# The stretch from the second norm to the first expert pair in a new order, with the normalised x gathered, and the last scatter by column halves

## The chip, the core and the metric

The kernel runs on one core of a Trainium2 chip. Its engines work beside each other, each through its own list of instructions: PE (TensorE, matrix products), DVE (VectorE), ACT (ScalarE), POOL (GpSimd), and SP (SyncE), which issues most of the transfers. They wait for one another by semaphores. The metric is the device time of one execution in microseconds (us), as a median of repeated runs.

## The reference

One decoder layer for 256 tokens with 1024 features: a mixer (a state-space branch and differential attention), cross-attention into 256 memory tokens, and a mixture of 64 experts. After each part x is normalised. What the change touches is the last third, cut here to what is computed:

```python
x = layer_norm(alpha * x + cross_attention(x, mem), ln2_g, ln2_b)       # the second norm
scores = sigmoid(x @ w_router); choice = scores + router_bias           # 64 experts in 8 groups of 8
grp_score = sum of the 2 largest choices in each group                  # the best 4 groups stay
idx = top 8 of choice inside those groups
gates = scores[idx] / sum(scores[idx]) * 2.5
y = (silu(x @ w_sh[:, :256]) * (x @ w_sh[:, 256:])) @ w_sh_down         # the shared expert
for e in range(64):
    gu = x @ w_gu[e]
    y += gates[:, e] * ((silu(gu[:, :256]) * gu[:, 256:]) @ w_down[e])
out = layer_norm(alpha * x + y, ln3_g, ln3_b)                           # the third norm
```

All numbers are float32. Where precision needs it, a float32 operand is split into a rounded part (`_hi`, `h`) and the rest (`_lo`, `l`), which PE multiplies in its faster form.

## The kernel before, in words

The tokens are two blocks of 128 (`TB`). PE goes through a fixed list of outputs, each 256 columns wide, in four PSUM banks S[0] to S[3] in turn (the tile name `stream` in the trace); four more banks W[0] to W[3] (`work`) take everything else. In the part that matters the order is written out by hand:

1. **Output projection** of the cross-attention, `token_major("co", k)`, eight outputs: the token block changes fastest, then the column block. DVE adds each to x (`add_output`, L1222) and takes statistics. When a token block is complete, DVE and ACT form its deviation (`variance`, `norm_sqrt`) and DVE normalises x in place (`normalise`, L1233, tile `xres`).
2. PE turns the normalised x of each token block (`turn`, L1747). Behind each turn it runs 13 products whose result nobody reads (`keep_warm`, L1587). ACT and DVE leave the turned x with the norm's gain and bias as `x2T` (L881, L1294).
3. **Router**: eight products for both token blocks at once (L1795), sigmoid on ACT, a turn on PE (L1802), and then the selection on DVE (L1307 to L1334), which ends with `sel`. Four products count the selected tokens (L1812), DVE makes places and one-hot matrices from the counts (L1350 to L1360). Meanwhile PE has the **shared expert's** four outputs (`token_major("sh", k)`, L1580).
4. In token layout, x gets its gain and bias by two operations a block: block 0 on DVE (`gain_bias`, L1251, L1252), block 1 on GpSimd (L652, L654). ACT rounds it (`x2h`, L891), DVE takes the rest (`x2l`, L1302).
5. **Gather**: products of `x2h`, `x2l` with the one-hot matrices (`gather`, L1827 to L1833) bring x to the experts' slots; ACT and DVE copy eight blocks out to `xg`. The products of the shared expert are turned in between (`turn_shared`, L1819).
6. **Pairs**: 32 pairs of experts. Of each, 32 records of gate and up (L1879), the scatter of the pair before (L1868; in pair 0 the shared expert's second product, L1854), turns, two blocks of the next gather, and the down products (L1903). ACT makes silu and `yh`, DVE `yl`. Pair 0 also adds the residual to the W banks (L1453, L1454), and ahead of it DVE lists overflow items (L1411 to L1427), which are none for this input.
7. **End**: the last scatter, the sums, and the third norm, whose first token block goes mainly through DVE and whose second goes through ACT (L946 to L956) and DVE (L1504 to L1511); two stores.

The expert weights come as 96 tiles of 2 MB in halves of 1 MB, on SP's queue, into a ring of 8 places (`places`). Place 6 is `place_w` and `place_x`; `place_x` shares its bytes with `xres`. Refills wait for PE's gate-up and down products (`refill`).

## Time and profile before

| | us |
|---|---|
| median of 3 runs (1011.42 to 1011.84) | 1011.68 |
| the profiled execution | 1012.25 |
| its span, first to last instruction | 1010.2 |
| PE busy | 987.0 |
| DVE busy | 517.0 |
| ACT busy | 382.7 |
| moved by DMA | 292.43 MB |

Times inside the trace count from the start of the span. The page gives busy time by engine; the chain of waits follows the end of the program back through what released what; a timeline lists the instructions of one engine in order, with the idle time ahead of each in brackets. "x8" behind a row is the number of instructions merged in it. The granted clock (PEclk) is a share of TensorE's full speed: 1.00 is 2.4 GHz, 0.50 is 1.2 GHz. PE, DVE and ACT work on different tiles at once, so a row's duration is only on the path where another engine waits for it.

### The profile page before, as it was taken

What the parts mean: (1) busy time and instruction counts of PE and PEld (TensorE: products, weight loads), DVE (VectorE), ACT (ScalarE), POOL (GpSimd) and SP (SyncE); (2) the same over time, 40 slices, a digit from 0 to 9 for tenths busy, and PEclk for the clock granted to TensorE, in tenths of its full rate; (3) what the DMA queues carried; (4) which work ended last, traced back from release to release, by engine and by line L of the source; (5) the groups of instructions that cost most, each with busy time, mean ns of one, the idle gap of its engine ahead of it and who ended that gap; (6) DMA issues with size and microseconds to landing.
All of it is one profiled execution on the core that took longest, in us unless ns stands there. A gap on an engine that the chain in (4) does not pass through costs nothing.

```text
span 1010.2 us, 15434 instructions
## 1 busy us (share of the span) xinstructions
PE 987.0 (98%) x6362; PEld 708.3 (70%) x6363; DVE 517.0 (51%) x1024; ACT 382.7 (38%) x705; POOL 58.6 (6%) x56
## 2 busy tenths in 40 slices
PE   8999999999999999999999999999999999999994
PEld 7999999999999999998874444444444444444332
DVE  5888456757589967845775232222223222322223
ACT  6776435555577735445321121111111111211112
POOL 0001103333200000000200000000000000000000
PEclk9999999999999999999999999999999999999998
DMA  7585534333344556559757999999999999999972
GB/s 295 189 307 181 194 128 165 126 125 126 126 170 164 195 182 227 190 209 390 277 208 286 416 420 419 420 420 420 420 420 420 419 420 421 421 419 420 420 320 84
DMA packets 42694, 292.43 MB, mean 289 GB/s; under 512 B 4728, under 2 KB 6912, under 8 KB 7936
## 3 DMA queue, kind: packets, MB, share of 16 engines
q1 hardware_dynamic: 41840, 286.19, 71.4%
q0 software_dynamic: 784, 5.24, 1.4%
q8 instruction: 51, 0.84, 0.3%
q14 instruction: 19, 0.16, 0.0%
HBM read 290.36 MB, written 2.63 MB: 290 GB/s over the span
## 4 chain that ended last, share of the span: by engine, by line
PE 94%; DVE 3%; ACT 1%; DMA 1%; issue 0%; SPq 0%; ACTq 0%
PE stream L1555 32%; PE stream L1879 22%; PE stream L1903 11%; PE stream L1580 8%; PE work L1868 7%; PE stream L1827 2%; PE stream L1831 1%; PE stream L1829 1%; PE stream L1833 1%; PE work L1678 1%; PE work L1654 1%; PE work L1854 1%; PE work L1767 1%; PE work L1781 1%; PE work L1666 1%; PE stream L1896 1%
## 5 line engine op out<-in xcount | busy, mean ns | idle before, releaser
L981 DVE TENSOR_TENSOR w_lo<-raw,w_hi 128x1024 fp32r<-128x1024 f32 x142 | 172.0, 1231 | 55.9 <-ACT w_hi L677 55.8
L1879 PE MATMUL stream<-ring,xg 128*64 128x512 f32 x640 | 197.0, 592 | 0.8 <-issue 0.8
L677 ACT ACTIVATE w_hi<-raw 128x1024 fp32r<-128x1024 f32 x142 | 147.1, 1052 | 61.3 <-DMA raw<-in_wdense 44.6
L1555 PE MATMUL stream<-xT_hi,w_hi 128*128 128x256 f32 x560 | 159.4, 285 | 0.0
L1555 PE MATMUL stream<-xT_lo,w_hi 128*128 128x256 f32 x560 | 157.9, 282 | 0.0
L1555 PE MATMUL stream<-xT_hi,w_lo 128*128 128x256 f32 x560 | 157.8, 282 | 0.0
L1879 PEld LDWEIGHTS stream<-ring,xg 128*64 128x64 f32 x640 | 63.0, 137 | 91.6 <-issue 90.4
L1555 PEld LDWEIGHTS stream<-xT_hi,w_hi 128*128 128x128 f32 x560 | 106.1, 190 | 3.7 <-issue 3.1
L1555 PEld LDWEIGHTS stream<-xT_hi,w_lo 128*128 128x128 f32 x560 | 105.9, 189 | 0.0
L1555 PEld LDWEIGHTS stream<-xT_lo,w_hi 128*128 128x128 f32 x560 | 105.6, 189 | 0.0
L1432 DVE TENSOR_TENSOR hh<-h,stream 128x256 f32<-128x256 f32 x32 | 13.5, 422 | 172.3 <-ACT h L910 172.3
L1459 DVE SCALAR_TENSOR_TENSOR yl<-stream,slot_gate,yh 128x512 fp32r<-128x512 f32 x64 | 48.0, 751 | 91.6 <-ACT yh L922 91.6
L910 ACT ACTIVATE h<-stream 128x256 f32<-128x256 f32 x32 | 12.3, 384 | 199.6 <-PE stream L1879 199.6
L922 ACT ACTIVATE yh<-stream,slot_gate 128x512 fp32r<-128x512 f32 x64 | 44.0, 687 | 101.0 <-PE stream L1903 101.0
L1903 PE MATMUL stream<-ring,hT 128*64 128x512 f32 x320 | 73.1, 598 | 1.3 <-DVE scatT L1439 1.3
L1879 PE MATMUL stream<-place_e,xg 128*64 128x512 f32 x128 | 56.2, 592 | 0.0
L1868 PE MATMUL work<-yh,scatT 128*128 128x512 f32 x128 | 53.7, 420 | 1.6 <-DVE yl L1459 1.6
L1868 PE MATMUL work<-yl,scatT 128*128 128x512 f32 x128 | 50.4, 394 | 0.0
L1903 PEld LDWEIGHTS stream<-ring,hT 128*64 128x64 f32 x320 | 21.2, 136 | 40.5 <-issue 34.3
L1868 PEld LDWEIGHTS work<-yh,scatT 128*128 128x128 f32 x128 | 24.0, 187 | 31.8 <-issue 25.1
L913 ACT ACTIVATE xg<-stream 128x512 f32<-128x512 f32 x28 | 16.7, 598 | 77.5 <-PE stream L1833 77.5
L1012 DVE SCALAR_TENSOR_TENSOR acc<-xpad,cs,acc 128x256 f32<-128x256 f32 x72 | 34.8, 484 | 2.4 <-ACT acc L713 0.7
(378 smaller groups left out, 2034.4 us busy)
## 6 DMA issues: line engine op xcount, KB each, us to landing
ring<-in_wstream SPq DMA_DIRECT2D x120, 1024.0 KB, 14.9
raw<-in_wdense SPq DMA_DIRECT2D x73, 1024.0 KB, 4.8
place_e<-in_wstream SPq DMA_DIRECT2D x24, 1024.0 KB, 16.0
place_m<-in_wstream SPq DMA_DIRECT2D x12, 1024.0 KB, 13.2
place_c<-in_wstream SPq DMA_DIRECT2D x12, 1024.0 KB, 14.9
place_w<-in_wstream SPq DMA_DIRECT2D x12, 1024.0 KB, 14.4
place_x<-in_wstream SPq DMA_DIRECT2D x12, 1024.0 KB, 16.0
ln<-in_lnp POOLq DMA_DIRECT2D x3, 1024.0 KB, 6.9
```

What stands on the lines that cost most here:

```text
L677: nc.scalar.activation(w_hi[:, q % ROUNDED, :], raw[:, q % 6, :], ACT.Copy).then_inc(w_rounded, 1)
L913: nc.scalar.activation(feature_block((pair // 4 + 1) % 2, 2 * (pair % 4)), S[1][:], ACT.Copy).then_inc(gath_act, 1)
L922: nc.scalar.activation(yh[:, c * 512:(c + 1) * 512], (S[3], S[1])[c][:], ACT.Copy, scale=slot_gate[:, 0:1]).then_inc(yh_done, 1)
L981: tt(w_lo[:, q % 6, :], raw[:, q % 6, :], w_hi[:, q % ROUNDED, :].bitcast(F32), ALU.subtract).then_inc(w_rest, 1)
L1012: ins = stt(acc[:, b % 2, :], xpad[:, b % 4, j:j + SEQ], conv_w[:, b, j:j + 1], acc[:, b % 2, :], ALU.mult, ALU.add)
L1459: stt(yl[:, c * 512:(c + 1) * 512], (S[3], S[1])[c][:], slot_gate[:, 0:1], yh[:, c * 512:(c + 1) * 512].bitcast(F32), ALU.mult, ALU.subtra ...
L1555: last = mm(S[n % 4][:, 0:SEQ], w[:, b, :], a[:, kb, :], start=(kb + j == 0), stop=(kb == chunks * KB - 1 and j == len(parts) - 1))
L1580: last = mm(S[n % 4][:, 0:SEQ], a[:, kb, rows], w[:, cols, :], start=(kb + j == 0), stop=(kb == KB - 1 and j == len(parts) - 1))
L1827: mm(by_expert[:, :, window[0]], x2h[:, 0, w], onehot[:, buf, 0, :, window[0]], start=True, stop=False, skip_group_check=True)
L1868: last = mm(W[2 * t + c][:], scatT[:, t * P:(t + 1) * P], y[:, c * 512:(c + 1) * 512], start=False, stop=False, skip_group_check=True)
L1879: last = mm(S[2][e * SLOTS:(e + 1) * SLOTS, :], feature_block(buf, kb)[:, col + e * SLOTS:col + (e + 1) * SLOTS], tiles[e][kb // 4][:, kb ...
L1903: last = mm((S[3], S[1])[c][e * SLOTS:(e + 1) * SLOTS, :], hT[:, kb, e * SLOTS:(e + 1) * SLOTS], tile[e][:, o:o + 512], start=(kb == 0), s ...
```

## The change

The edits, most of them between the second norm and the first pair:

- The output projection runs its eight outputs in another order (`ORDER`), so that token block 0 is complete at the sixth. The turn of block 0 stands inside the eighth output, the turn of block 1 inside the shared expert's first output. The shared expert's outputs are ordered by token block. `keep_warm` is gone from here.
- The router's products are made for each token block by itself, in two bands of the array, four features' blocks each; a product with a matrix of two identities adds the bands and turns the scores. The sigmoid comes after that.
- The gathered x is the normalised x without gain and bias (`xn_hi`, `xn_lo`). Gain and bias are applied when ACT and DVE leave the gathered banks (`leave_gathered`). The token layout gets its gain and bias on DVE just ahead of pair 0; GpSimd has no part in it any more.
- The selection has fewer operations (one masked operation for both blocks, one product with `lower8`).
- The count stands inside the shared expert's last output. DVE makes the gates after the one-hots.
- The first gather takes its banks in another order (`first_banks`); the first half of the first pair waits for four of the eight blocks.
- The residual is added in four operations rather than eight. The list of overflow items moves behind pair 1.
- The first half of expert tile 6 is loaded earlier, its second half after the residual. The shared expert's second weight (`wsd`) is loaded once the last shared output is done, to other bytes.
- In each pair ACT copies the turned h ahead of the gathered block.
- The last scatter goes by column halves. A root of one element is computed in the last pair, ahead of `yh`.
- The third norm's second block is subtracted, scaled and stored by halves.

```diff
+ORDER = {"co": [(0, 0), (1, 0), (0, 1), (1, 1), (0, 2), (0, 3), (1, 2), (1, 3)],
+         "sh": [(0, 0), (0, 1), (1, 0), (1, 1)]}
...
+    return ORDER[kind][k] if kind in ORDER else (k % TB, k // TB)
...
+        DONE.append(OUT0[_k] + 1 + (last_output(_k, _m, _q // 2) if _k in TOKEN_MAJOR else _q // _c))
...
-            sp.wait_ge(split_l, 2)
-            expert_halves(6, 6)
+            expert_half(6, 6, 0)
             sp.wait_ge(proj_ready, DONE[-1])
             expert_halves(7, 7)
...
+                if pair == 0:
+                    sp.wait_ge(residual_done, 4)
+                    expert_half(6, 6, 1)
...
+            for c in range(2):
+                cols = slice(c * 512, (c + 1) * 512)
+                sp.wait_ge(ln_done, TB + 2 + c)
+                sp.dma_start(out[0, P:SEQ, cols], normed[:, 1, cols]).then_inc(stored, 16)
...
-            nc.gpsimd.tensor_tensor(xres[:, 1, :], xres[:, 1, :], ln2[:, 0, :], ALU.mult).then_inc(norm_pool, 1)
...
+            pool.wait_ge(proj_ready, DONE[-1])
             pool.dma_start(wsd[:], wshd).then_inc(wsd_ld, 16)
...
+                if t == 0:
+                    round_x(0)
...
+            round_x(1)
+            act.wait_ge(router_mm, 2)
+            nc.scalar.activation(scoresT[:], W[0][:, 0:SEQ], ACT.Copy).then_inc(score_sig, 1)
+            act.wait_ge(router_mm, 3)
+            nc.scalar.activation(scores[:], W[3][:, 0:TB * EXPERTS].rearrange("p (t e) -> p t e", t=TB), ACT.Sigmoid
+                                 ).then_inc(score_sig, 1)
...
+            def leave_gathered(buf, kb, bank):
+                nc.scalar.activation(feature_block(buf, kb), bank[:], ACT.Identity, scale=gain2[:, kb:kb + 1],
+                                     bias=gain2[:, KB + kb:KB + kb + 1]).then_inc(gath_act, 1)
...
+                if pair == PAIRS - 1:
+                    nc.scalar.activation(half_var[:, 1:2], ones[:, 0:1], ACT.Sqrt)
...
+            add_output("co", {6: lambda: normalise(1, 0).then_inc(xhat_done, 1), 7: lambda: leave_x2T(0)})
+            normalise(1, 1).then_inc(xhat_done, 1)
+            leave_x2T(1)
...
-            link(ts(gmask[:], goff[:], TOP_GROUPS - 0.5, None, ALU.is_lt))
-            link(ts(goff[:], gmask[:], -MASKED, MASKED, ALU.mult, ALU.add))
-            for t in range(TB):
-                by_group = masked[:, t].rearrange("p (g e) -> p g e", g=EGROUPS)
-                link(tt(by_group, choice[:, t].rearrange("p (g e) -> p g e", g=EGROUPS),
-                        gmask[:, t].unsqueeze(2).to_broadcast([P, EGROUPS, 8]), ALU.mult))
-                link(tt(by_group, by_group, goff[:, t].unsqueeze(2).to_broadcast([P, EGROUPS, 8]), ALU.add))
+            link(ts(gmask[:], goff[:], TOP_GROUPS - 0.5, 0.5, ALU.is_lt, ALU.subtract))
+            link(stt(masked[:].rearrange("p t (g e) -> p t g e", g=EGROUPS),
+                     gmask[:].unsqueeze(3).to_broadcast([P, TB, EGROUPS, 8]), -4.0 * MASKED,
+                     choice[:].rearrange("p t (g e) -> p t g e", g=EGROUPS), ALU.mult, ALU.min))
...
+            shared_product(0)
+            ve.wait_ge(router_mm, 4)
...
+            shared_product(1)
...
+            def gain_bias(t):
+                link(tt(xres[:, t, :], xres[:, t, :], ln2[:, 0, :], ALU.mult))
+                link(tt(xres[:, t, :], xres[:, t, :], ln2[:, 1, :], ALU.add))
+            ve.wait_ge(ln_ld, 32)
+            for t in range(TB):
+                gain_bias(t)
...
-                            link(stt(bank, x2h[:, t, cols].bitcast(F32), ALPHA, bank, ALU.mult, ALU.add))
-                            stt(bank, x2l[:, t, cols].bitcast(F32), ALPHA, bank, ALU.mult, ALU.add
-                                ).then_inc(residual_done, 1)
+                            stt(bank, xres[:, t, cols], ALPHA, bank, ALU.mult, ALU.add).then_inc(residual_done, 1)
...
+                if pair == 1:
+                    list_items()
...
+                    if t:
+                        ve.wait_ge(norm_act, 5 + c)
...
+            subtract_third_mean(1)
+            ve.wait_ge(ln_sqrt, 2 * TB + 2)
+            link(nc.vector.reciprocal(rstd[:, 1:2], half_var[:, 0:1]))
+            for c in range(2):
+                cols = slice(c * 512, (c + 1) * 512)
+                stt(normed[:, 1, cols], normed[:, 1, cols], rstd[:, 1:2], ln3[:, 1, cols], ALU.mult, ALU.add
...
-                keep_warm(S[0][:, 0:SEQ], ocT_r[0][:, 0, 0:P], ocT_r[0][:, 1, :], 13)
...
+            def scores_of(t):
+                pe.wait_ge(x2T_act, 4 * t + 4)
+                pe.wait_ge(x2T_dve, 4 * t + 4)
+                for step in range(4):
+                    for band in range(2):
+                        kb = 4 * band + step
+                        last = mm(W[0][band * EXPERTS:(band + 1) * EXPERTS, t * P:(t + 1) * P], w_router[:, kb, :],
+                                  x2T[:, kb, t * P:(t + 1) * P], start=(step == 0), stop=(step == 3))
+                last.then_inc(router_mm, 1)
...
+                    last = mm(W[3][:, t * EXPERTS:(t + 1) * EXPERTS], scoresT[:, t * P:(t + 1) * P], two_ident[:],
+                              start=True, stop=True)
...
+            for k in range(8):
+                token_major("co", k, ocT_r, ready=(cav_rest, 2) if k == 0 else None,
+                            midway={1: lambda: turn_normed(0)} if k == 7 else {})
+            scores_of(0)
+            token_major("sh", 0, x2T, midway={6: lambda: turn_normed(1)})
+            token_major("sh", 1, x2T, midway={3: lambda: scores_of(1), 6: turn_scores})
             token_major("sh", 2, x2T)
-            pe.wait_ge(sel_done, 1)
-            for k, (w, t) in enumerate(((tri, 0), (tri, 1), (ones, 0), (ones, 1))):
-                last = mm(W[2][:, k * EXPERTS:(k + 1) * EXPERTS], w, sel[:, t, :], start=True, stop=True)
-            last.then_inc(router_mm, 1)
-            token_major("sh", 3, x2T)
+            token_major("sh", 3, x2T, midway={4: count_selected})
...
+                if kb in (0, 2):
+                    turn_shared(kb // 2)
                 elif kb >= 4:
                     pe.wait_ge((gath_act, gath_dve)[kb % 2], (kb - 4) // 2 + 1)
-                gather(kb, S[kb % 4], 0)
+                gather(kb, first_banks[kb], 0)
...
+                    if pair % 4 == 0:
+                        pe.wait_ge(gath_act, 2 + pair + 2 * half)
+                        pe.wait_ge(gath_dve, 2 + pair + 2 * half)
...
+            def scatter_half(c, y):
+                for t in range(TB):
+                    mm(W[2 * t + c][:], scatT[:, t * P:(t + 1) * P], y[:, c * 512:(c + 1) * 512], start=False, stop=False,
+                       skip_group_check=True)
+            pe.wait_ge(yl_done, 2 * PAIRS - 1)
+            scatter_half(0, yh)
+            scatter_half(0, yl)
+            pe.wait_ge(yh_done, 2 * PAIRS)
+            scatter_half(1, yh)
             pe.wait_ge(yl_done, 2 * PAIRS)
-            scatter()
+            scatter_half(1, yl)
```

Where the instructions move, two places on PE and one on ACT. On PE, between the output projection and the shared expert, before (L1747 turns x, L1587 is the part nobody reads, L1795 the router, L1580 the shared expert, `ocT` the input of the output projection):

```order
L1747 MATMUL work<-cs,xres 128x128 [waits xhat_done,dve_took]
L1747 MATMUL work<-cs,xres 128x128 x7
L1587 MATMUL stream<-ocT_hi 128x256 x13
L1747 MATMUL work<-cs,xres 128x128 [waits xhat_done]
L1747 MATMUL work<-cs,xres 128x128 x7
L1587 MATMUL stream<-ocT_hi 128x256 x13
L1795 MATMUL work<-x2T,cs 64x256 [waits x2T_dve,x2T_act]
L1795 MATMUL work<-x2T,cs 64x256 x7
L1580 MATMUL stream<-raw,x2T 128x256 [waits dense_ld0,dve_took]
L1580 MATMUL stream<-raw,x2T 128x256 x3
L1802 MATMUL work<-cs,scoresT 128x64 [waits score_sig]
L1802 MATMUL work<-cs,scoresT 128x64
```

And now, from the first router products on (L1830); the turn of block 0 is further up, inside the last output of the projection:

```order
L1830 MATMUL work<-x2T,cs 64x128 [waits x2T_dve,x2T_act]
L1830 MATMUL work<-x2T,cs 64x128 x7
L1616 MATMUL stream<-raw,x2T 128x256 [waits dense_ld0,dve_took]
L1616 MATMUL stream<-raw,x2T 128x256 x3
L1616 MATMUL stream<-raw,x2T 128x256 [waits dense_ld0]
L1616 MATMUL stream<-raw,x2T 128x256
L1783 MATMUL work<-cs,xres 128x128 [waits xhat_done]
L1783 MATMUL work<-cs,xres 128x128 x7
L1616 MATMUL stream<-raw,x2T 128x256 x2
L1616 MATMUL stream<-raw,x2T 128x256 [waits dense_ld1,dve_took]
L1616 MATMUL stream<-raw,x2T 128x256 x2
L1830 MATMUL work<-x2T,cs 64x128 [waits x2T_dve,x2T_act]
```

The router's products are half as wide and come twice, each between pieces of other products, and both turns have moved into such pieces.

On PE, from the count of the selected to the gather, before (L1812 the count, L1580 the last shared output, L1819 the turn of the shared product) and, in the second piece, now (L1844, L1616, L1859):

```order
L1812 MATMUL work<-sel,cs 128x64 [waits sel_done]
L1812 MATMUL work<-sel,cs 128x64 x3
L1580 MATMUL stream<-raw,x2T 128x256 [waits dve_took]
L1580 MATMUL stream<-raw,x2T 128x256 x7
L1819 MATMUL work<-cs,hh 128x128 [waits sh_done,split_l,onehot_done]
L1819 MATMUL work<-cs,hh 128x128
L1827 MATMUL stream<-onehot,x2h 128x8x48 [waits sh_silu]
```

```order
L1616 MATMUL stream<-raw,x2T 128x256 x3
L1844 MATMUL work<-sel,cs 128x64 [waits sel_done]
L1844 MATMUL work<-sel,cs 128x64 x3
L1616 MATMUL stream<-raw,x2T 128x256 x4
L1859 MATMUL work<-cs,hh 128x128 [waits sh_done,split_l,onehot_done]
L1859 MATMUL work<-cs,hh 128x128
L1867 MATMUL stream<-onehot,xn_hi 128x8x48
```

The count is inside an output, and the gather's first blocks no longer wait for ACT's second silu.

On ACT, from the last pair's silu to the end, before and now (`half_var` of L943 is the root of one element; the rows between the branches, which run only for overflow items, are among them):

```order
L910 ACTIVATE h_191<-stream 128x256 [waits gu_mm]
L916 ACTIVATE hT<-stream 128x256 [waits hT_mm]
L922 ACTIVATE yh<-stream,slot_gate 128x512 [waits down_mm,gate_cp]
L922 ACTIVATE yh<-stream,slot_gate 128x512 [waits down_mm]
...
L929 ACTIVATE h_191<-stream 128x256 [waits o_gu]
...
L946 ACTIVATE unread,half_sum<-work 128x512 [waits moe_mm]
L946 ACTIVATE unread,half_sum<-work 128x512 [waits norm_act]
L948 ACT_TABLE_LOAD [waits ln_var]
L948 ACTIVATE rstd<-rvar 128x1 [waits norm_act]
L949 ACTIVATE half_sum<-half_sum 128x1
```

```order
L934 ACTIVATE h_193<-stream 128x256 [waits gu_mm]
L936 ACTIVATE hT<-stream 128x256 [waits hT_mm]
L943 ACT_TABLE_LOAD
L943 ACTIVATE half_var<-cs 128x1
L947 ACTIVATE yh<-stream,slot_gate 128x512 [waits down_mm,gate_cp]
L947 ACTIVATE yh<-stream,slot_gate 128x512 [waits down_mm]
...
L954 ACT_TABLE_LOAD
L954 ACTIVATE h_193<-stream 128x256 [waits o_gu]
...
L971 ACT_TABLE_LOAD
L971 ACTIVATE unread,half_sum<-work 128x512 [waits moe_mm]
L971 ACTIVATE unread,half_sum<-work 128x512 [waits norm_act]
L973 ACT_TABLE_LOAD [waits ln_var]
L973 ACTIVATE rstd<-rvar 128x1 [waits norm_act]
```

There is a table load ahead of the root of one element, one inside the branch, one ahead of the first sum (L971), and one ahead of the root of the third norm (L973), where before there was one, at L948.

## Rows read from the trace of the kernel before

**Rows 1.** The page: busy time, share of the span and instructions of each engine.

```profile
PE 987.0 (98%) x6362; PEld 708.3 (70%) x6363; DVE 517.0 (51%) x1024; ACT 382.7 (38%) x705; POOL 58.6 (6%) x56
```

**Rows 2.** Windows: stretch, length, busy us by engine, PEclk, DMA share, GB/s.

```profile
700.00:714.50 14.50, 14.50 (x70) 6.62 (x69) 4.50 (x12) 2.63 (x5) 0.00 (x0) 1.00 1.02 422
...
1003.00:1006.00 3.00, 0.00 (x0) 0.00 (x0) 1.93 (x4) 0.94 (x4) 0.00 (x0) 0.50 0.43 175
```

**Rows 3.** Chain of waits, output projection: start us, us, what.

```profile
471.51 22.42 PE stream L1580 x192
```

**Rows 4.** Timeline of PE: start us, us, engine, line, op, out<-in, shapes [idle before].

```profile
494.01 1.07 PE L1747 MATMUL work<-cs,xres 128*128 128x128 f32 x8
494.83 1.80 PE L1587 MATMUL stream<-ocT_hi 128*128 128x256 f32 x13
...
505.12 8.90 PE L1580 MATMUL stream<-raw,x2T 128*128 128x256 f32 x40
513.86 1.00 PE L1812 MATMUL work<-sel,cs 128*128 128x64 f32 x8
514.70 3.67 PE L1580 MATMUL stream<-raw,x2T 128*128 128x256 f32 x16
...
520.86 0.44 PE L1819 MATMUL work<-cs,hh 128*128 128x128 f32 x2 [0.51 <-DVE hh L1383]
...
521.84 0.34 PE L1827 MATMUL stream<-onehot,x2h 128*128 128x384 f32 x1
...
525.39 0.35 PE L1827 MATMUL stream<-onehot,x2h 128*128 128x384 f32 x1
...
527.09 1.47 PE L1879 MATMUL stream<-ring,xg 128*64 128x512 f32 x5 [0.83 <-issue]
```

**Rows 5.** Groups by line, PE: xcount | busy us, mean ns | idle.

```profile
L1678 PE MATMUL work<-dec,xsdt 128*64 128x128 f32 x128 | 8.8, 279 | 0.0
```

**Rows 6.** Timeline of DVE from the second norm to the one-hots.

```profile
493.95 0.42 DVE L1222 SCALAR_TENSOR_TENSOR xres<-xres,stream 128x256 f32<-128x256 f32 x1
...
495.85 0.81 DVE L1233 TENSOR_SCALAR xres<-xres,mv,rstd 128x1024 f32<-128x1024 f32 x1 [0.27 <-ACT rstd L841]
...
501.48 3.25 DVE L1252 TENSOR_TENSOR xres<-xres,ln 128x1024 f32<-128x1024 f32 x1
...
505.44 0.28 DVE L1308 TENSOR_TENSOR choice<-work,row 128x128 f32<-128x128 f32 x1
...
509.24 0.17 DVE L1325 TENSOR_SCALAR goff<-gmask 128x16 f32<-128x16 f32 x1
...
511.65 0.23 DVE L1334 TENSOR_SCALAR sel<-choice 128x128 f32<-128x128 f32 x1
...
513.34 1.22 DVE L1302 TENSOR_TENSOR x2l<-xres,x2h 128x1024 fp32r<-128x1024 f32 x1
...
515.16 0.22 DVE L1350 TENSOR_SCALAR over<-work 128x64 f32<-128x64 f32 x1
...
516.32 1.03 DVE L1360 TENSOR_TENSOR onehot<-cs,slot_of 128x384 fp32r<-128x384 f32 x2
```

**Rows 7.** All transfers of L514 from 519 us on: issue to landing.

```profile
DMA to landing us min/median/max: 4.8/15.2/24.7
```

**Rows 8.** Chain of waits at the end, and the page's row on the stores.

```profile
994.13 0.70 ACT yh L922
...
995.66 2.13 PE work L1868 x8
...
999.90 1.28 ACT L948
...
1004.03 1.41 DVE normed L1504 x2
...
1005.55 1.28 DVE normed L1511
...
out_dram<-normed SPq DMA_DIRECT2D x2, 512.0 KB, 2.6
```

263 lines of the change are left out of this document (114 added, 149 removed).

## The prediction

> **What bounds the kernel now.** I read the page first: PE is busy 987.0 of 1010.2 us [rows 1], so only the places where PE waits, or does work that can go, are worth anything. Then the table of windows: a stretch inside the 32 expert pairs shows PE busy 14.50 of 14.50 us while the DMA share is 1.02 at 422 GB/s [rows 2]. That is two limits almost at once, and I return to it. Then the chain of waits [rows 3]: the output projection of the cross-attention starts at 471.51 and holds it for 22.42 us. The first expert product starts at 527.09 [rows 4]. The changed stretch is these 55.6 us. Last the timelines of PE and DVE between these marks [rows 4, 6]. DVE goes without a break from the router's scores (choice at 505.44) over the selection (sel at 511.65), the places (515.16) and the one-hot matrices (516.32), and PE can begin its gather only when DVE and ScalarE have handed over everything. So between the second norm and the gather a chain through DVE sets the time, not PE.
>
> **The stretch, rebuilt step by step.** I lay PE's new program on the clock of the profiled execution.
>
> The output projection: 22.42 us from 471.51 [rows 3] ends at 493.93. The new order of its eight outputs finishes the first 128 tokens at output 5. In the trace the add of a last column block starts at 493.95 and the normalised x of that token block ends at 496.66 (495.85 + 0.81) [rows 6]: 2.71 us of DVE and ScalarE. From the end of output 5 (493.93 minus two outputs of 2.80, 22.42 / 8, is 488.33) that gives 491.1, and PE wants it at 491.5, one eighth into output 7. So the turn of x (eight transposes) goes inside output 7 without a wait. It costs PE 0.82 (from 494.01 to the next product at 494.83 [rows 4]): 494.75. ScalarE rounds x first and then leaves its four x2T blocks, which I estimate at 2.5 us together, by 493.7, before PE asks.
>
> Scores of the first half: eight products of 64 weight columns by 128, in two bands of the array. The trace has this very shape: x128 in 8 batches, 8.8 us busy [rows 5], 1.10 a batch. To 495.85. In the kernel before all eight came as 256-column products, after both halves were ready. Lower bound 0.87 (pairs of products on the two bands side by side at full overlap), upper bound 1.75 (no overlap).
>
> Shared expert, output 0: records follow each other at 0.2185 us (8.74 us for 40, from 505.12 to 513.86) [rows 4], 16 of them are 3.5; with the second turn inside, 500.15. The second half of x is normalised 2.71 after 494.8, at 497.5; PE asks at 498.5. Output 1: 3.5, plus 1.10 for the second scores, plus the product that adds the two bands and turns the scores. That product is half of the four at 513.86 (0.84 to the next row at 514.70), 0.42. It ends at 505.15. Outputs 2 and 3 up to the middle: 508.65, 510.4.
>
> Does the selection keep up? PE is at the second scores at 501.45 and leaves them at 502.55; ScalarE copies them (0.4), then must load the sigmoid's table, 1.28 us by the load at 999.90 [rows 8]; it stands behind the copy, where before it stood ahead of the wait for the scores. That ends near 504.3, while PE has turned the scores at 504.25. Sigmoid 0.4: DVE starts choice at about 504.75, 0.7 earlier than 505.44. From there to sel before: 511.65 + 0.23 - 505.44 = 6.44. Gone are five small links (four masked operations and goff, from 509.24 to 510.49, now one operation of 0.3) and one geq link (0.2): -1.15. So sel is ready at 510.05; PE reaches the count at 510.4. A margin of 0.35 us, thin. Before, the DVE work that followed sel (gates, one x2l of 1.22 at 513.34, zeros) sat ahead of the places; now it is done while DVE waited for scores, or behind the one-hots.
>
> Count 0.84: 511.25. Places and one-hots: 515.16 to 516.32 and 1.03 more [rows 6], 2.2 us: 513.5. PE ends the last shared output at 513.0, so a wait of 0.5 us stays. Gather: a transpose pair with its block costs 0.98 (520.86 to 521.84), a block alone 0.71 (five blocks from 521.84 to 525.39) [rows 4]. Two by 0.98 and six by 0.71 is 6.2: 519.7. The first expert product then waited 0.83 us for the last gathered blocks to leave their banks [rows 4]; now it asks for four of the eight, long done, and for the others 3.4 us later. Leaving a bank now multiplies and adds the norm's gain; it is off the path with 0.5 us or more at each bank. Start of the first pair: 519.7. **Saved: 527.09 - 519.7 = 7.4 us.**
>
> **Inside the pairs** nothing is gained: PE issues the same products, 14.50 of 14.50 busy. In pair 0 DVE now does gain and bias on x (four operations) where it listed the overflow items. Before, such an operation took 3.25 us at 501.48, with GpSimd working on the other half of x; the subtraction of the same size took 1.22 at 513.34, with GpSimd idle [rows 6]. I take 1.22, 4.9 us in all, and the list that leaves was about as long. At 3.25 each it would be 13, and h would be late by about 2 us for PE in pair 0. The Trainium skill (SBUF — State Buffer, Who interferes with whom) says that a DVE operation with two SBUF inputs and a GpSimd one that reads SBUF lock each other out; by that rule the new place, with GpSimd idle, is cheap. Residual adds halve, four by 0.7.
>
> The transfers: half of expert tile 6 now goes into the bytes of x, so it is issued only after the residual adds. By pairs of 14.5 us [rows 2] and about 5.5 more in pair 0 for the shared product, that is some 20 us behind pair 0's start (my estimate), and pair 2 needs it 3.4 us into its own products, at 29 + 5.5 + 3.4 = 38. Landings took 4.8 to 24.7 us in this stage, median 15.2 [rows 7]: 15.2 leaves 3 us, and at that point of the stage the queue is still short. Value: nothing; bound: 24.7 gives a wait of 6.7. The queue also carries 1 MB more (2.5 us at 422 GB/s) while it is nearly full.
>
> **The end.** The last scatter was eight products behind the last yl, from 995.66, 2.13 us with the two that close the sums [rows 8]. Six of the eight now need only what is there before, and two are left: at about 0.235 each (2.13 less 0.25 for the closing two, by eight) six are 1.4. The third norm's second half: its two subtractions (1.41 at 1004.03) now start one by one behind the squares and are done at about the time the root ends, and the last scaling (1.28 at 1005.55) is cut in two of 0.65, the same in sum: 1.41 less the reciprocal and a link is 1.05 gained. The last store is 256 KB in place of 512 KB at 2.6 us [rows 8]; between nothing and half of it I take 0.4. **The table of the root:** the title says that it is loaded in the last pair. Yet the order of ScalarE's instructions shows behind it a load ahead of the copy that sums (L971) and again one ahead of the root (L973), as before at 999.90, 1.28 us. So this gains nothing, and adds one load of 1.28, which fits: from ScalarE's last yh (994.13 + 0.70 [rows 8]) with a branch to about 996.2, against the banks ready at 997.8 - 1.4 = 996.4. The Trainium skill (ScalarE activation tables: per-element evaluation and per-set limits, Table sets in the compiler and the runtime) says that loads are placed per block, which agrees with that order: a branch stands between. Another page of the Trainium skill (ScalarE: Activation LUTs, What ACT_TABLE_LOAD costs) adds a drain of 1.38 us to each load; by it the end would be some 0.7 later; the chain of waits has nothing but the load's 1.28 there, and speaks against it. **Saved at the end: 1.4 + 1.05 + 0.4 = 2.8 us.**
>
> **Sum.** 7.4 + 2.8 = 10.2. The profiled execution took 1012.25 (span 1010.2 and 2.0 around it), 0.57 above the median of the runs, so it goes to 1002.05 and the median from 1011.68 to **1001.5**.
>
> **Rivals.**
> - The selection is late. If DVE misses the count slot (margin 0.35), all behind it slips: scores without overlap (+1.3), or a slower chain. Time 1002.5 to 1004. For it: three hand-overs on ScalarE and PE within 3 us. Against: PE then also has less to wait for.
> - The transfers become the bound. A wait in pair 2 for tile 6, up to 6.7, or late in the stage, where the rate of 422 GB/s (14.9 us for the 6.29 MB of a pair) is below PE's 14.5: the lead shrinks each pair. Time 1003 to 1008.2.
> - Pair 0's DVE work is late (2 us): 1003.5.
> - The root's load does leave the path: 1.3 less, 1000.2. The order speaks against it.
> - **Slower than before:** the 26 warming products (L1587) go. If PE's clock fell to its lower level (the granted clock is 0.50 at 1003 to 1006, when PE had been idle since its last product near 997.8 [rows 2, 8]) through a gap at the one-hots, the work under it would double: one pair adds 14.5 us, and from 10.2 us of work at half clock the change loses; 1016 with one pair. Against: the granted clock is 1.00 before inside the pairs, which follow a gap of 0.83 us and one of 0.51 [rows 2, 4], and the new waits are no longer.
>
> **How the numbers follow.** Forecast 62%; selection late 17%; transfers 8%; pair 0 late 4%; load gone 5%; clock 2%; and 2% that nothing of it comes through (1011.7). The range of 8 in 10: from 1000.2 (load gone, scores at their lower bound) to 1005.0 (selection late and a part of the transfers). A measurement tells 0.2%, 2.0 us, from no change. Faster 96%, same 2%, slower 2%.
>
> **What would show it.** The first L1918 product near 519.7; the first gathers with about 0.5 us of idle time, released by the one-hots; no idle time at the count; no wait for DMA at pair 2; PE 14.5 a pair; two loads of 1.28 on ScalarE behind the last yh; the two last products at 0.1 behind yl; the last store about 8 us behind the banks (before 1005.55 + 1.28 against 997.8, 9.0). It is wrong if PE waits at the count, at a bank in the gather or in the pairs, or if the clock falls.

## The result, and the profile after

The changed kernel took 1002.50 us (median of four runs, 1001.78 to 1003.16) against 1011.71 for the kernel before (four runs, 1011.42 to 1011.84): ratio 0.9901, 95% interval 0.9880 to 0.9922. The forecast was 1001.5 with a range from 1000.2 to 1005.0. It was faster, as forecast, by 9.2 us where I had said 10.2.

The page of the changed kernel, against [rows 1]: the span is 10.4 us shorter, PE's busy time 6.2.

```profile
span 999.8 us, 15421 instructions
...
PE 980.8 (98%) x6354; PEld 702.5 (70%) x6355; DVE 517.1 (52%) x1019; ACT 392.1 (39%) x709; POOL 53.0 (5%) x54
```

The two profiled spans do not differ by the change alone. The start of PE's timeline (columns: start us, us, engine, line, op, out<-in, shapes, x instructions, [idle before]), before and after:

```profile
6.60 5.77 PE L1555 MATMUL stream<-xT,raw 128*128 128x256 f32 x14 [0.80 <-DMA raw<-in_wdense]
```

```profile
6.48 5.85 PE L1591 MATMUL stream<-xT,raw 128*128 128x256 f32 x25 [0.67 <-DMA raw<-in_wdense]
```

Both rows stop at 12 us, where the view's window ends. The code is the same there, but up to that mark PE has started 14 products in one case and 25 in the other. The trace's record of the granted clock says why: it rises from 0.50 to 1.00 (1.2 to 2.4 GHz) at 11.66 us before and at 5.82 us after. Up to the output projection that leaves the two kernels 1.38 us apart, a matter of the run and not of the change, as more traces show below.

The stretch on PE, to be held against [rows 4]:

```profile
490.10 1.03 PE L1783 MATMUL work<-cs,xres 128*128 128x128 f32 x8
...
493.51 1.09 PE L1830 MATMUL work<-x2T,cs 128*64 128x128 f32 x16
494.54 2.86 PE L1616 MATMUL stream<-raw,x2T 128*128 128x256 f32 x12
497.23 1.04 PE L1783 MATMUL work<-cs,xres 128*128 128x128 f32 x8
...
500.36 1.09 PE L1830 MATMUL work<-x2T,cs 128*64 128x128 f32 x16
...
502.78 0.55 PE L1837 MATMUL work<-two_ident,scoresT 128*128 128x64 f32 x4
503.18 6.26 PE L1616 MATMUL stream<-raw,x2T 128*128 128x256 f32 x28
509.27 1.00 PE L1844 MATMUL work<-sel,cs 128*128 128x64 f32 x8
510.11 1.95 PE L1616 MATMUL stream<-raw,x2T 128*128 128x256 f32 x8
512.56 0.44 PE L1859 MATMUL work<-cs,hh 128*128 128x128 f32 x2 [0.51 <-DVE onehot L1379]
...
518.83 5.37 PE L1918 MATMUL stream<-ring,xg 128*64 128x512 f32 x24
```

Read the start and the brackets. PE goes from the output projection, whose last output holds the turn at 490.10, through scores, shared expert and count (509.27) to the gather with one idle time only, 0.51 us for the one-hot matrices at 512.56. Where [rows 4] had 0.83 us ahead of the first pair, the first pair starts at 518.83 with none. VectorE, to be held against [rows 6]:

```profile
503.69 0.29 DVE L1333 TENSOR_TENSOR choice<-scores,row 128x128 f32<-128x128 f32 x1 [1.07 <-ACT scores L906]
...
508.66 0.23 DVE L1354 TENSOR_SCALAR sel<-choice 128x128 f32<-128x128 f32 x1
...
510.31 0.23 DVE L1369 TENSOR_SCALAR over<-work 128x64 f32<-128x64 f32 x1 [0.97 <-PE work L1844]
...
511.48 1.03 DVE L1379 TENSOR_TENSOR onehot<-cs,slot_of 128x384 fp32r<-128x384 f32 x2
...
523.58 1.22 DVE L1431 TENSOR_TENSOR xres<-xres,ln 128x1024 f32<-128x1024 f32 x1
...
528.61 1.03 DVE L1379 TENSOR_TENSOR onehot<-cs,slot_of 128x384 fp32r<-128x384 f32 x2
529.56 0.41 DVE L1462 TENSOR_TENSOR hh<-h,stream 128x256 f32<-128x256 f32 x1
```

Now the selection waits for its input (1.07 us at 503.69) and the places for the count (0.97 at 510.31): the chain through VectorE stands beside PE's work. It is done with sel at 508.89 (508.66 + 0.23), 0.38 us before PE starts the count. Gain and bias take 1.22 us each at 523.58, as in the subtraction at 513.34 of [rows 6] and not as at 501.48. The second group's one-hots and h (528.61, 529.56) follow.

The tail, against [rows 8]:

```profile
983.42 2.75 PE L1942 MATMUL stream<-ring,hT 128*64 128x512 f32 x12
...
987.12 0.63 PE L1987 MATMUL work<-yh,scatT 128*128 128x512 f32 x2
987.12 1.28 ACT L971 ACT_TABLE_LOAD   x1 [0.22 <-issue]
...
987.74 0.72 PE L1987 MATMUL work<-yl,scatT 128*128 128x512 f32 x2
...
989.02 0.38 PE L1900 MATMUL work<-onehot,turner 128*128 128x2 f32 x2 [0.56 <-issue]
...
991.39 1.28 ACT L973 ACT_TABLE_LOAD   x1 [0.54 <-DVE rvar L1237]
...
992.99 1.28 DVE L1541 SCALAR_TENSOR_TENSOR normed<-normed,rstd,ln 128x1024 f32<-128x1024 f32 x1 [0.37 <-ACT rstd L973]
...
995.95 1.42 DVE L1547 SCALAR_TENSOR_TENSOR normed<-normed,rstd,ln 128x512 f32<-128x512 f32 x2
996.73 0.99 SPq L621 DMA_DIRECT2D out_dram<-normed  x2
```

The two last scatter products (987.74) stand 0.05 us behind the last yl, but ahead of the closing sums is an idle time marked issue, 0.56 us at 989.02. Behind its last yh ScalarE loads two tables, one at 987.12 under cover and one at 991.39 on the chain of waits.

From the marks of the two traces (first product of the output projection, of the first pair, end of the last down product, end of the span) the difference of 10.42 us divides so. (The first product has its own record a little ahead of the merged row: 471.16 against the 471.51 of [rows 3].)

| stretch | before | after | gain | forecast |
|---|---|---|---|---|
| start to output projection | 471.16 | 469.78 | 1.38 | 0 |
| output projection to first pair | 55.93 | 49.04 | 6.89 | 7.4 |
| pairs, to the end of the last down product | 466.99 | 467.34 | -0.35 | 0 |
| tail | 16.15 | 13.65 | 2.50 | 2.8 |
| of it: from the last down product to the end of the closing sums | 3.82 | 3.24 | 0.58 | 1.4 |
| third norm, to VectorE's last instruction | 8.93 | 7.96 | 0.97 | 1.05 |
| last store | 3.41 | 2.45 | 0.96 | 0.4 |

What went from PE in the stretch can be counted in the two traces. Two rows of the timeline before and one of its chain of waits belong to it:

```profile
497.57 1.79 PE L1587 MATMUL stream<-ocT_hi 128*128 128x256 f32 x13
...
519.24 0.41 PE L1819 MATMUL work<-cs,hh 128*128 128x128 f32 x2 [0.87 <-DVE hh L1383]
```

```profile
499.37 3.64 PE work L1795 x16
```

From the start of each record to the start of the next, the 26 unread products took 3.6 us and are gone; the router's products took 3.57 and take 2.05, 1.5 less; and PE's idle time falls from 2.4 us (0.1, 0.1, 0.87, 0.51, 0.83) to 0.51, 1.9 less. That is the 6.9 us, but for 0.1. So most of it is work that PE no longer does. No run puts the unread products back, so their price by itself is read from the rows and not measured.

### The profile page after: what moved, and what is told of

Its sections match the earlier page's. It is cut to its first block, busy times and chain, and to the rows that moved or that the text cites. A ratio compares the mean times of both kernels' runs of the same rounds, so it can differ in the third digit from the quotient of the medians.

```text
span 999.8 us, 15421 instructions
## 1 busy us (share of the span) xinstructions
PE 980.8 (98%) x6354; PEld 702.5 (70%) x6355; DVE 517.1 (52%) x1019; ACT 392.1 (39%) x709; POOL 53.0 (5%) x54
## 4 chain that ended last, share of the span: by engine, by line
PE 95%; DVE 2%; DMA 1%; ACT 0%; issue 0%; SPq 0%; DVEq 0%; ACTq 0%
PE stream L1591 32%; PE stream L1918 22%; PE stream L1942 11%; PE stream L1616 9%; PE work L1907 6%; PE stream L1867 2%; PE stream L1871 1%; PE stream L1869 1%; PE stream L1873 1%; DMA raw<-in_wdense 1%; PE work L1714 1%; PE work L1690 1%; PE work L1893 1%; PE work L1803 1%; PE work L1817 1%; PE work L1702 1%
## 5 line engine op out<-in xcount | busy, mean ns | idle before, releaser
L936 ACT ACTIVATE hT<-stream 128x256 f32<-128x256 f32 x32 | 12.3, 384 | 92.1 <-PE stream L1935 92.1
L1404 DVE TENSOR_SCALAR xg<-stream,gain 128x512 f32<-128x512 f32 x32 | 25.8, 810 | 23.2 <-PE stream L1873 23.2
## 6 DMA issues: line engine op xcount, KB each, us to landing
place_m<-in_wstream SPq DMA_DIRECT2D x12, 1024.0 KB, 15.2
```

Source lines behind the costliest of these rows:

```text
L1404: return ts(dst, src, gain2[:, kb:kb + 1], gain2[:, KB + kb:KB + kb + 1], ALU.mult, ALU.add)
```

## The experiments

All kernels of a group ran on one chip with runs of the kernel before. The differences asked for are mostly one or two us, and the runs of one kernel lie 0.2 to 1.5 us apart, in seven of the kernels (before among them) 2 to 4.4, so each verdict goes by the marks of its one trace, and the time stands beside it. The columns below are those of the table above. Beside the tail, the stretch alone, the early count and the 6 products, before took 1012.13 us (13 runs); in the two other groups 1011.87 and 1011.89 (7 each).

| kernel | time, median (range) | full clock from | projection starts | stretch | pairs | tail |
|---|---|---|---|---|---|---|
| before | 1011.71 | 11.66 | 471.16 | 55.93 | 466.99 | 16.15 |
| changed | 1002.50 | 5.82 | 469.78 | 49.04 | 467.34 | 13.65 |
| tail alone | 1009.86 (1008.89 to 1010.37) | 10.92 | 470.73 | 55.93 | 467.30 | 13.89 |
| stretch alone | 1005.02 (1004.10 to 1006.73) | 6.47 | 469.80 | 49.09 | 467.35 | 15.78 |
| count of items early | 1001.79 (1000.99 to 1001.92) | 10.24 | 470.50 | 49.08 | 467.28 | 12.84 |
| 6 products at the start | 1001.91 (1001.73 to 1001.94) | 7.37 | 469.96 | 48.96 | 467.35 | 13.65 |
| root behind the branch | 1001.58 (1001.42 to 1002.32) | 5.63 | 469.69 | 49.11 | 467.36 | 13.22 |
| no root in the pair | 1002.41 (1001.89 to 1003.33) | 10.29 | 470.55 | 49.04 | 467.34 | 13.64 |
| selection later | 1004.62 (1004.46 to 1007.32) | 10.27 | 470.48 | 51.01 | 467.37 | 13.65 |
| bands in turn | 1004.23 (1002.81 to 1007.05) | 11.53 | 474.22 | 49.88 | 467.32 | 13.67 |
| old order | 1004.73 (1003.90 to 1008.11) | 5.51 | 469.76 | 52.81 | 467.23 | 13.64 |
| items before the pairs | 1006.69 (1004.41 to 1006.73) | 11.14 | 470.92 | 48.95 | 471.04 | 13.65 |
| gain before choice | 1007.23 (1006.63 to 1008.73) | 10.03 | 470.38 | 53.60 | 467.36 | 13.64 |
| three edits | 1000.66 (1000.58 to 1000.91) | 5.54 | 469.89 | 49.15 | 467.37 | 12.39 |

**The two halves of the change, each alone.** The tail in the kernel before, and the stretch with the tail of before:

```diff
 # tail alone: before, with
+            pe.wait_ge(yl_done, 2 * PAIRS - 1)
+            scatter_half(0, yh)
+            scatter_half(0, yl)
+            pe.wait_ge(yh_done, 2 * PAIRS)
+            scatter_half(1, yh)
             pe.wait_ge(yl_done, 2 * PAIRS)
-            scatter()
+            scatter_half(1, yl)
 # and the third norm by halves, three stores, the Sqrt in the last pair
 # stretch alone: the changed kernel with all of these back as before
```

> The kernel before with the tail of the change alone: last scatter by column halves, third norm by halves, store in three pieces, the unneeded Sqrt in the last pair. Theory (parts are independent): from the end of the last down product to the end of the span 13.6 us as in the changed kernel, where before has 16.1; time 1009.2 us (1011.7 - 2.5), start and stretch as before. Rival (the tail gains only because pairs and stretch before it shifted): the tail stays over 15 us and the time over 1010.7.

> The changed kernel with the tail of before. Theory: from the first co product to the first product of pair 0 48.6 us (before 55.6), tail 16.1 us, time 1011.7 - 7.0 + 0.3 = 1005.0 us where PE's clock is granted late at the start and 1003.7 where early. Rival (the parts depend on one another): stretch or tail off these by over 0.5 us.

The tail alone gives 13.89, with stretch 55.93 and so no share in the rest; the stretch alone gives 49.09 and keeps 15.78. Without the last store the tails are 11.08 against 11.20 of the changed kernel and 12.74 against 12.74 of before, so each part is worth the same, within 0.12, with or without the other, and the times follow (1009.86 against 1012.13 of before beside it, 1005.02 against the same; -2.3 and -7.1). The rivals fall. Two more things come out. The pairs of before, in the first of these, take 467.30, so the 0.35 us that the changed kernel seemed to lose there belongs to the one trace of before (most of its full pairs take 14.53 us, in the tail alone and in the changed kernel they take 14.55). And the last store, in one piece of 512 KB, takes 3.41 and 3.04 us in two traces; in two pieces it takes 2.44 to 2.46 in eleven traces and 2.81 in the one of the tail alone. What the two pieces are worth lies between 0.2 and 1.0, mostly at 0.6 to 1.0, not at one number.

**Where the scatter's gain went.** What stands ahead of the branch on overflow items is moved, on PE:

```diff
+            pe.wait_ge(items_ld, 32)
+            n_items = pe.value_load(items[0:1, P:P + 1], min_val=0, max_val=EXTRA)
             pe.wait_ge(yl_done, 2 * PAIRS - 1)
             scatter_half(0, yh)
...
             scatter_half(1, yl)
-            pe.wait_ge(items_ld, 32)
-            n_items = pe.value_load(items[0:1, P:P + 1], min_val=0, max_val=EXTRA)
             with pe.If(n_items > 0):
```

> The changed kernel, with TensorE's wait for the list of overflow items and its load of their number moved ahead of the last scatter. Theory (this load is what lies exposed between the last scatter product and the end sums, 0.56 us idle marked issue): the idle goes, banks are ready 2.6 us after the last down product instead of 3.13, time -0.5 us. Rival (the branch itself costs the time, not the load): idle stays at 0.4 to 0.6 us, time unchanged.

The end of PE's timeline:

```profile
988.43 0.74 PE L1987 MATMUL work<-yl,scatT 128*128 128x512 f32 x2
989.01 0.28 PE L1900 MATMUL work<-onehot,turner 128*128 128x2 f32 x2
```

The idle time is gone: the closing sums start 0.58 us behind the last pair of scatter products, where it was 1.28 (987.74 to 989.02). From the end of the last down product to that of the closing sums it is 2.43 us, not 3.24: 0.81 gained, 0.70 between these two starts and 0.10 in the closing sums themselves (0.38 to 0.28). With before's 3.82 that makes 1.39, the 1.4 that the prediction had for the scatter. The traces also record the load and the branch, which the rows above leave out. Before, PE's queue starts the load with the first of the eight scatter products (995.68) and is through the branch at 996.78, while the products run on to 997.8. In the changed kernel it starts the load with the last two (987.74) and is through the branch at 988.96, 0.06 ahead of the closing sums. With the load moved, only the branch, 0.36 us, is left beside the last two. So the rival, that the branch itself costs the time, falls.

**The start.**

```diff
-            keep_warm(W[3][:, 0:SEQ], xpad[:, 0, 0:P], xpad[:, 1, 0:SEQ], 4)
+            keep_warm(W[3][:, 0:SEQ], xpad[:, 0, 0:P], xpad[:, 1, 0:SEQ], 6)
```

> The changed kernel with 6 unread products instead of 4 at the start, so that TensorE does not idle before the first projection product at 6.5 us. Theory (1.3 us of the gain seen in the profiled run, and the two values 1002 and 1003.2 of the changed kernel's runs, are the moment at which the full clock is granted, 5.8 or 11.7 us, and not the change): the records show full clock by 7 us, all runs at 1001.8 to 1002.2, none at 1003. Rival (the moment does not depend on TensorE's idle time at the start): runs still split 1.2 us apart, or all 0.2 to 0.8 us later for the added products.

Full clock came at 7.37 us, with no idle time ahead of it, and the four runs lie within 0.21 us. The theory holds in its first part: the table above has twelve traces with the same code at the start and two with 6 products, and where full clock comes late (10 to 11.7 us) the output projection starts at 470.4 to 471.2, where early (5.5 to 7.4) at 469.7 to 470.0, changed kernel or not (the 474.2 of "bands in turn" has another cause, below). That the two products made it early is not shown: with 6 it was early in both traces (the other is "three edits", 5.54), and the eight runs lie within 0.21 and 0.33 us, but with 4 it was early in four traces of twelve as well. Nor does the idle time ahead of the first projection product tell them apart: it was 0.67 us with an early rise in the changed kernel, 0.68 with a late one in "items before the pairs", and 0.92 with an early one in "root behind the branch".

**The table of the root.** First the Sqrt is moved behind the branch, then it is left out:

```diff
                 if pair < LAST_GROUP:
                     leave_gathered(...)
-                if pair == PAIRS - 1:
-                    nc.scalar.activation(half_var[:, 1:2], ones[:, 0:1], ACT.Sqrt)
...
+            nc.scalar.activation(half_var[:, 1:2], ones[:, 0:1], ACT.Sqrt)      # root behind the branch only
             act.wait_ge(moe_mm, 2)
```

> The changed kernel, with the unneeded Sqrt moved from the last pair to behind the branch on overflow items, ahead of ScalarE's wait for the banks. Theory (the load of 1.28 us in front of the first root lies on the path because the load behind the branch takes another table; whatever is run first behind the branch chooses the table): one load behind the branch, done before the banks are ready, none at the first root; from the banks' end to the last scaling 6.7 us instead of 7.96, time -1.25 us. Rival (two loads stay, since the sum that follows brings its own table back): time unchanged or +0.2.

> The changed kernel without the unneeded Sqrt in the last pair. Theory (it loads a table that the branch makes the next instruction load over, so it does nothing): the loads behind the branch and at the first root stay, tail 13.65 us, time unchanged within 0.3 us. Rival (it is what lets the load behind the branch be covered): the third norm 1.28 us longer.

Left out, the tail stays, 13.64, and so does the load at the root (992.15). The two other loads of the changed kernel's end, at 982.29 in the last pair and at 987.12 behind the branch, are both gone, where I expected the second to stay: that Sqrt brought them, and both were under cover. It did nothing for the end. Moved, one load is left, and the tail is 13.22, a gain of 0.43 where I expected 1.25. ScalarE and VectorE in that kernel:

```profile
987.12 1.28 ACT L967 ACT_TABLE_LOAD   x1 [0.22 <-issue]
...
991.25 1.39 DVE L1534 SCALAR_TENSOR_TENSOR normed<-work,neg_mean,ln 128x512 f32<-128x512 f32 x2
991.43 0.20 ACT L972 ACTIVATE rstd<-rvar 128x1 f32<-128x1 f32 x1 [0.56 <-DVE rvar L1236]
...
992.68 1.28 DVE L1540 SCALAR_TENSOR_TENSOR normed<-normed,rstd,ln 128x1024 f32<-128x1024 f32 x1
...
993.88 1.40 DVE L1534 SCALAR_TENSOR_TENSOR normed<-work,neg_mean,ln 128x512 f32<-128x512 f32 x2
993.94 0.29 ACT L980 ACTIVATE half_var<-half_square 128x1 f32<-128x1 f32 x1
...
995.51 1.42 DVE L1546 SCALAR_TENSOR_TENSOR normed<-normed,rstd,ln 128x512 f32<-128x512 f32 x2
```

The root comes at 991.43 instead of 992.69, 1.26 earlier, and the squares' root ends at 994.23. But VectorE is busy from 991.25 to the end of its second subtraction, 995.28, with breaks of no more than 0.04 us: 1.39, 1.28 and 1.40 in a row, and only then comes the last scaling. The changed kernel's own trace says how little there was to gain. VectorE waits for ScalarE in two places only, 0.37 us for the root ahead of the scaling at 992.99, and some 0.1 us inside the second subtraction, which takes 1.52 us there and 1.40 here. The squares' root was ready at 995.50, before VectorE got to it at 995.75. The Trainium skill (ScalarE: Activation LUTs, What ACT_TABLE_LOAD costs) gives 1283 ns for a load and 1380 ns more for a drain. The load agrees, 1.28 here; of the drain these traces show nothing: in the changed kernel's trace the load at 991.39 ends at 992.67 and the root starts at 992.69.

**The margin of the selection.**

```diff
             link(nc.vector.tensor_reduce(goff[:], gcmp[:], AX.X, ALU.add))
+            link(nc.vector.tensor_reduce(goff[:], gcmp[:], AX.X, ALU.add))      # six times more
```

> The changed kernel with the reduction that forms goff run seven times instead of once, 6 x 0.32 = 1.9 us of VectorE's work more ahead of the selection. Theory (TensorE's own work sets the stretch, the selection is 0.38 us ahead of the count): TensorE now waits 1.55 us at the count, stretch 49.04 -> 50.6 us, time +1.5 us. Rival 1 (VectorE's chain sets the stretch through the wait for the one-hot rows): +1.9 us. Rival 2 (the margin is larger): under 1 us.

```profile
511.61 1.10 PE L1850 MATMUL work<-sel,cs 128*128 128x64 f32 x8 [1.43 <-DVE sel L1360]
...
515.00 0.44 PE L1865 MATMUL work<-cs,hh 128*128 128x128 f32 x2 [0.51 <-DVE onehot L1385]
```

PE waits 1.43 us at the count (1.55 expected) and 0.51 at the one-hots as before: that much is the theory. Counted from the projection's start sel is done 1.97 us later (the six operations are 1.93 of it) and the count begins 1.64 us later; the margin, 0.33 by this and 0.38 by the trace, swallowed the rest. But the whole stretch is longer by 1.97: 0.1 more between the count and the one-hots and 0.2 in the gather, at a bank that VectorE frees. By its total this is rival 1; by its waits, the theory with what it left out. A margin of 0.38 us covers the wait at the count only; the bank further on had none.

**The scores in two bands.**

```diff
-                for step in range(4):
-                    for band in range(2):
+                for band in range(2):
+                    for step in range(4):
```

> The changed kernel with the router's products of one band all ahead of those of the other, instead of in turn. Theory (two products into different bands of the array overlap, which is why 16 passes take 1.03 us): each block's scores take 1.7 us, TensorE's stretch +1.3 us. Rival (passes of 128 columns overlap in any order): stretch unchanged within 0.2 us.

```profile
497.81 1.58 PE L1830 MATMUL work<-x2T,cs 128*64 128x128 f32 x16
```

16 passes take 1.58 us instead of 1.09, twice 0.49, and the stretch grows by 0.84, where I expected 1.3. The overlap of the two bands is real and needs them alternated; I had put the cost of each block 0.1 too high (1.7). The trace starts its output projection at 474.22, 3.1 us behind the latest of the others: one weight chunk landed 6.7 us after its issue (median 5.1), VectorE got to its rest at 456.49 where the changed kernel's trace has 453.20, and the granted clock was 0.50 from 465.5 to 468.9, behind four idle times of PE of 0.22, 0.67, 0.67 and 0.52 us where every other trace has two (0.63 and 0.52). All of it lies ahead of the edit. The other runs of this kernel were 2.7 to 4.2 us shorter.

**What the order of the projection's outputs is worth.**

```diff
-ORDER = {"co": [(0, 0), (1, 0), (0, 1), (1, 1), (0, 2), (0, 3), (1, 2), (1, 3)],
-         "sh": [(0, 0), (0, 1), (1, 0), (1, 1)]}
+ORDER = {"sh": [(0, 0), (0, 1), (1, 0), (1, 1)]}
...
-            add_output("co", {6: lambda: normalise(1, 0).then_inc(xhat_done, 1), 7: lambda: leave_x2T(0)})
+            add_output("co", {7: lambda: normalise(1, 0).then_inc(xhat_done, 1)})
+            leave_x2T(0)
...
-                token_major("co", k, ocT_r, ready=(cav_rest, 2) if k == 0 else None,
-                            midway={1: lambda: turn_normed(0)} if k == 7 else {})
+                token_major("co", k, ocT_r, ready=(cav_rest, 2) if k == 0 else None)
+            turn_normed(0)
```

> The changed kernel with the co outputs in the order of before (token block fastest), so that token block 0 is complete only with output 6, its normalisation stands ahead of output 7 on VectorE, and its turn behind output 7 on TensorE. Theory (the new order hides block 0's turn and the leaving of its transposed copy beside output 7): TensorE waits 2.1 us for x2T ahead of the first scores, stretch 49.04 -> 51.2 us, time +2.1 us. Rival (what was freed ahead of the selection and the first pair is all that counts, the order nothing): stretch within 0.3 us of 49.04.

```profile
495.59 1.09 PE L1830 MATMUL work<-x2T,cs 128*64 128x128 f32 x16 [1.97 <-DVE x2T L1313]
```

```profile
496.00:502.00 6.00, 6.00 (x34) 4.96 (x31) 0.16 (x1) 0.37 (x2) 0.00 (x0) 0.72 0.94 397
```

(Columns of the second: stretch, its length, busy us of PE, PEld, DVE, ACT, POOL, PEclk, DMA share, GB/s.) PE waits 1.97 us for x2T, near the 2.1 expected. But the stretch grows by 3.77. Behind the wait the granted clock is 0.50 from 497.03 to 500.45, which the window shows as 0.72, and 3.41 us at half clock are 1.7 us lost. 1.97 + 1.7 is 3.7. The trace is that of the run of 1005.40 us; two others (1003.90, 1004.06) are some 1.4 below it and may have gone without the fall, but no trace of them shows it.

**What was freed ahead of the first pair and ahead of the selection.** `list_items()` back from pair 1 to the place ahead of pair 0; and the four gain and bias operations from behind the gather to the place ahead of the selection:

```diff
+            list_items()                 # items before the pairs
             for pair in range(PAIRS):
...
-                if pair == 1:
-                    list_items()
 # gain before choice
             rest_of_x(1)
+            ve.wait_ge(ln_ld, 32)
+            for t in range(TB):
+                gain_bias(t)
             ve.wait_ge(score_sig, 2)
```

> The changed kernel with the list of overflow items (some 5.4 us of VectorE's small operations) back ahead of pair 0. Theory (TensorE needs the second group's one-hot rows at 533.0 us, VectorE has them at 529.6, so 3.4 us of the 5.4 are covered): TensorE waits 2.0 us in pair 0, from the first gate-up product to the last down product 467.34 -> 469.4 us, stretch unchanged, time +2.0 us. Rival (the wait is made up again in later pairs, or the cover holds all of it): time within 0.5 us.

> The changed kernel with the four gain and bias operations (4 x 1.25 us on VectorE, same data) back ahead of the selection. Theory (gathering the normalised x pays because these operations leave VectorE's chain ahead of the count): VectorE is free at 507.6 instead of 502.6 us where the selection could start at 503.7, so the count is 3.9 - 0.4 = 3.5 us late, with 0.2 to 0.4 us behind it; stretch 49.04 -> 52.7 us, time +3.6 us. Rival (TensorE's work alone sets the stretch, selection has cover): under 1 us.

```profile
536.25 0.44 PE L1866 MATMUL stream<-onehot,xn_hi 128*128 128x384 f32 x1 [2.05 <-DVE onehot L1379]
...
537.26 0.63 PE L1934 MATMUL stream<-cs,hh 128*128 128x128 f32 x2
```

```profile
536.00:542.00 6.00, 5.75 (x22) 3.41 (x24) 4.21 (x12) 1.38 (x3) 0.61 (x2) 0.72 0.02 4
```

And, with the gain before the choice:

```profile
513.40 1.10 PE L1844 MATMUL work<-sel,cs 128*128 128x64 f32 x8 [3.37 <-DVE sel L1362]
```

Both waits stand where and as long as the theory had them: 2.05 us at the second group's one-hots (2.0 expected), 3.37 at the count (3.5). Both totals are above it, 3.70 for 2.0 and 4.56 for 3.7, and again the records have half clock for 3.41 us behind the wait (536.79 to 540.21, and 515.20 to 518.61), 1.7 us each. 2.05 + 1.7 is 3.7; 3.37 + 1.7 less the 0.51 at the one-hots, which is gone, is 4.6. So each of the two moves is needed for itself: undone, it costs 2.05 and 3.37 us of waiting, and in both traces the clock on top. The gain and bias operations take 1.22 or 1.23 us each in this place too, where the kernel before had 2.31 and 3.25 for them with GpSimd at work on the other block, so the short time goes with GpSimd at rest and not with the place. But this kernel does not restore the old arrangement, in which GpSimd had half of them: there VectorE was through with its half at 504.73 and then stood 0.50 us for the scores, so they held the selection up in no way.

**The three edits together**, count of items early, root behind the branch, 6 products at the start:

> The changed kernel with three edits together: TensorE's load of the overflow count ahead of the last scatter, the unneeded Sqrt behind the branch instead of in the last pair, 6 unread products at the start. Theory (the three lie at different places and add up): tail 13.65 - 0.81 - 0.45 = 12.4 us, start as in the run with 6 products, span 998.6 us, time 1000.6 us. Rival (with the banks 0.8 us earlier the table load behind the branch, done at 988.4 us, or VectorE's own work takes their place): tail 12.8 to 13.2 us, time 1001 to 1001.5.

Tail 12.39 (12.4 expected), 1000.66 us, all four runs within 0.33. The table load behind the branch, at 987.37 to 988.65, ends 0.2 us ahead of the banks: little room is left in it. The ratio to before is 0.9889 (0.9872 to 0.9905), and the median is 1.8 us below the changed kernel's; those two were not run beside each other, but no run of one reaches those of the other (1000.91 at most, 1001.78 at least), and the tail is 1.26 shorter in the traces.

## Why the prediction came true, and where not

**Right in mechanism, place by place.** In the changed kernel PE's own work sets the stretch; there is no idle time at the count; the first gather waits 0.51 us for the one-hots (0.5 said); the first pair starts without a wait; pair 2 waits for no transfer; gain and bias take 1.22 each; the loads of ScalarE are where the order put them; the last two scatter products are 0.05 behind yl. In the clock of the trace of before (1.38 added) sel comes at 510.27 (510.05 said), the count at 510.65 (510.4), the one-hots at 513.89 (513.5), the first pair at 520.2 (519.7). The 0.5 us that the stretch gave less grew in small steps from end to end: 0.14 by the first scores, 0.25 by the count, 0.4 by the one-hots.

**The reading it began with** is half right: that before the change a chain through VectorE set this stretch, not PE. PE stood idle 2.4 of its 55.9 us, and the rest of the wait for the normalised x and its turned copies was filled with 3.6 us of unread products. At the count nothing waited: sel was done at 511.88, PE came at 513.86. The chain came last only at the shared expert's turn (519.24, 0.87 us). The new order takes those waits away and does without the filling; "old order", which has no filling either, shows 1.97 us of such a wait, with the fall of the clock behind it.

**The transfer for tile 6** was issued 19.5 us behind the first pair's start (20 said) and landed at most 7.3 us later, where the prediction took 15.2: the room was some 10 us, not 3. PE's list of waits names no transfer in the pairs.

**The margin of the selection**, 0.35 said, is 0.38. Three experiments show how little it holds: 1.97 us more ahead of sel cost PE 1.43 us of waiting, the gain and bias operations 3.37, and with the old order PE waits 1.97 already at the first scores.

**The scatter's 1.4** is the step that failed: 0.58. I counted matrix products and not what PE's queue has to do behind them, the load of the count and the branch. With the load ahead of the scatter it is 1.39.

**The last store's 0.4** is 0.96 in the profiled pair, 0.2 to 1.0 over all traces; my bound of half of 2.6 holds. The two misses, 0.8 too much at the scatter and 0.6 too little at the store, nearly cancel in the tail, and that is luck.

**The root's load.** It stays on the path, as said. But the rival priced its leaving at 1.3 us, and it is worth 0.43: I read from the chain of waits that the load lay on it, not how long VectorE would have been busy without it. The 0.7 us that the prediction names for a drain do not follow from its rows, and no trace shows a drain.

**The rival of the clock** did not come true: the granted clock stays 1.00 through the stretch, where PE's longest wait is 0.51. The mechanism is real in other kernels here, but its price was wrong by far: after a wait of 1.97 to 3.37 us half clock lasted 3.41 us in three traces and cost 1.7, not the 14.5 of a pair.

**The sum.** 6.9 + 2.5 = 9.4 in the traces, less the 0.35 of the pairs 9.0; the medians say 9.2. The profiled executions show 10.2, by luck what I forecast: 1.4 of it is the start.

## What to carry to other kernels

Before a gain between two traces is given to a change, line them up at a mark ahead of it: 1.4 of 10.4 us here lay where nothing was changed. When an edit shortens what runs on an engine, ask what that engine's queue did meanwhile (a load of a count, a branch): it becomes the next wait. When a step is taken from a chain, look how long the engine at its end stood idle for it: 0.37 us, and 0.1 at a second place, of a root that came 1.26 us earlier. And when an engine is busy throughout, ask which of its work has a reader: 3.6 of the 6.9 us here were products that only filled waits.
